# Filter spectra with half of the transforms, and the rest as sums and differences

## The reference

```python
z_pos, window = hyena_pos_features(L)
spec = hyena_filter_spectra(z_pos, window, hy_w1[i], hy_b1[i], hy_w2[i], hy_b2[i],
                            hy_w3[i], hy_b3[i], hy_freq[i])
y_b = hyena_mixer(hy, hy_conv[i], spec, hy_skip[i]) @ w_br_hyena[i]
```

## Time and profile before

| | |
|---|---|
| median of 3 runs | 2994.93 us (2990.47 to 2996.48) |
| profiled execution | 2988.92 us |
| its span | 2987.1 us |
| mean granted TensorE clock | 0.967 |
| TensorE, VectorE, ScalarE, GpSimd busy | 94%, 67%, 51%, 2% |
| stage `spectra` in the span | about 1634.8 to 1696.9 us |

### The profile page before, as it was taken

The page is one execution under the profiler, slowest core; times in us unless marked ns, Lnnn a source line. Parts: engine busy times, 40 slices in busy tenths (PEclk is TensorE's granted clock), DMA queues, the critical chain, the costliest instruction groups (busy, mean ns, idle before and its releaser), DMA issues. The chain is left out here.

```text
span 2987.1 us, 43738 instructions
## 1 busy us (share of the span) xinstructions
PE 2808.3 (94%) x17891; PEld 2482.1 (83%) x17891; DVE 2004.8 (67%) x2003; ACT 1514.4 (51%) x1456; POOL 68.8 (2%) x55
## 2 busy tenths in 40 slices
PE   5899998699999999999998989999899899989999
PEld 5799998588888888888886578999899788989898
DVE  6555565588888888888785466665555666666555
ACT  3444353466667676667663325444434326443442
POOL 1000000000000000000000210000000110000000
PEclk8899989699999999999999899999999999999999
DMA  6155540399999999999997234444355433444353
GB/s 188 61 180 192 177 155 16 121 365 331 368 329 349 347 334 364 328 366 334 340 356 233 94 97 127 142 155 142 113 178 190 147 111 102 150 147 141 127 186 110
DMA packets 365125, 619.40 MB, mean 207 GB/s; under 512 B 14664, under 2 KB 201127, under 8 KB 363701
## 3 DMA queue, kind: packets, MB, share of 16 engines
q1 hardware_dynamic: 363432, 611.77, 59.8%
q10 hardware_dynamic: 1550, 5.57, 0.5%
HBM read 611.93 MB, written 5.37 MB: 207 GB/s over the span
## 5 line engine op out<-in xcount | busy, mean ns | idle before, releaser
L366 DVE TENSOR_TENSOR slots_low<-slots,w_hi 128x2048 fp32r<-128x2048 f32 x240 | 549.5, 2293 | 379.4 <-ACT w_hi L355 379.2
L355 ACT ACTIVATE w_hi<-slots 128x2048 fp32r<-128x2048 f32 x240 | 452.8, 1891 | 335.9 <-PE ps L940 170.9
L1267 DVE TENSOR_TENSOR slots_low<-slots,w_hi 128x2048 fp32r<-128x2048 f32 x224 | 504.2, 2286 | 65.1 <-ACT w_hi L1218 65.1
L468 PE MATMUL ps<-x_hi,w_hi 128*128 128x256 f32 x1520 | 438.7, 289 | 51.5 <-DVE x_lo L548 26.7
L468 PE MATMUL ps<-x_lo,w_hi 128*128 128x256 f32 x1520 | 431.7, 284 | 0.0
L468 PE MATMUL ps<-x_hi,slots_low 128*128 128x256 f32 x1520 | 431.1, 284 | 0.0
L1218 ACT ACTIVATE w_hi<-slots 128x2048 fp32r<-128x2048 f32 x224 | 415.9, 1907 | 0.1
L1151 PE MATMUL ps<-slots_low,x_hi 128*128 128x512 f32 x896 | 352.1, 393 | 0.0
L468 PEld LDWEIGHTS ps<-x_hi,w_hi 128*128 128x128 f32 x1520 | 295.9, 195 | 59.4 <-issue 52.2
L468 PEld LDWEIGHTS ps<-x_lo,w_hi 128*128 128x128 f32 x1520 | 295.6, 194 | 0.3
L468 PEld LDWEIGHTS ps<-x_hi,slots_low 128*128 128x128 f32 x1520 | 295.3, 194 | 0.0
(11 more groups left out here) (536 smaller groups left out, 5374.0 us busy)
## 6 DMA issues: line engine op xcount, KB each, us to landing
slots<-in_moe_w_gate_dram SPq DMA_DIRECT2D x112, 1024.0 KB, 5.1
slots<-in_moe_w_up_dram SPq DMA_DIRECT2D x112, 1024.0 KB, 5.1
slots<-in_moe_w_down_dram SPq DMA_DIRECT2D x112, 1024.0 KB, 4.9
slots<-in_mlp_w_dram SPq DMA_DIRECT2D x64, 1024.0 KB, 5.2
slots<-in_w_in_dram SPq DMA_DIRECT2D x54, 1024.0 KB, 5.4
slots<-in_ffn_w_gate_dram SPq DMA_DIRECT2D x14, 1024.0 KB, 5.0
slots<-in_ffn_w_up_dram SPq DMA_DIRECT2D x14, 1024.0 KB, 5.0
slots<-in_ffn_w_down_dram SPq DMA_DIRECT2D x14, 1024.0 KB, 4.9
```

The costliest lines, as they stand in the source:

```text
L355: act.activation(w_hi[:, s.buffer, 0:s.kt * s.cols], slots[:, s.slot, 0:s.kt * s.cols], ACT.Copy).then_inc(w_hi_done, 1)
L366: dve.tensor_tensor(slots_low[:, s.slot, 0:n], slots[:, s.slot, 0:n], w_hi[:, s.buffer, 0:n].bitcast(F32), ALU.subtract).then_inc(w_lo_don ...
L468: mm = pe.matmul(b[:, t * T:(t + 1) * T], w, xx[:, k, :], **flags)
L1267: dve.tensor_tensor(low[i % NS], raw[i % NS], his[i % R].bitcast(F32), ALU.subtract).then_inc(lo_done, 1)
```

## The change

In a transform of the mirrored frequencies only the sign of the part over the odd (or even) tokens differs. The changed kernel no longer adds even and odd in a bank. `transform(i, s, t)` is one product for cosines or sines (s) over even or odd tokens (t), for the first 128 frequencies alone, into a bank of its own. ScalarE copies the even part of each into `evens`, which lies in the memory of `x_lo`, free in this stage. VectorE makes the sum and the difference of the odd part (in its bank) and the even part into `spectra` (`join`). `join(i, 0)` stands ahead of `mix(i + 1)` and of the size in VectorE's queue, `join(i, 1)` behind the size. The clearing of one row goes from VectorE to GpSimd, ahead of its addition.

```diff
-        xl = sb(ctx, "x_lo", [P, KD, T], F32R)
+        x_lo_plain, xl = pinned(ctx, "x_lo", [P, KD, T])
...
-                        def transform(i, n):
-                            s, k = n // 2, n % 2
+                        def transform(i, s, t):
                             pe.wait_ge(mixed, 2 * i + s + 1)
                             if i:
-                                pe.wait_ge(outed, 4 * (i - 1) + n + 1)
-                            for t in range(TT):
-                                mm = pe.matmul(bank(4 + n), dft[:, t, s, k * P:(k + 1) * P], pq[i % 2][:, s, t, :], start=(t == 0), stop=(t == TT - 1))
-                            mm.then_inc(transformed, 1)
+                                if t == 0:
+                                    pe.wait_ge(evens_out, 2 * (i - 1) + s + 1)
+                                else:
+                                    pe.wait_ge(joined, 4 * (i - 1) + 2 * s + 2)
+                            pe.matmul(bank(4 + 2 * s + t), dft[:, t, s, 0:P], pq[i % 2][:, s, t, :], start=True, stop=True).then_inc(transformed, 1)
...
                         def add_up(i):
                             pe.wait_ge(added, i + 1)
                             if i:
-                                pe.wait_ge(outed, 4 * i)
+                                pe.wait_ge(joined, 4 * i)
...
-                            transform(i, 0)
-                            transform(i, 1)
+                            transform(i, 0, 0)
+                            transform(i, 0, 1)
                             add_up(i)
-                            transform(i, 2)
+                            transform(i, 1, 0)
                             pe.wait_ge(sized, i + 1)
-                            transform(i, 3)
+                            transform(i, 1, 1)
...
-                            dve.wait_ge(windowed, 4 * i + 4)
-                            dve.memset(fb[0:1, 1, 0, :], 0.0).then_inc(lag0, 1)
...
+                        def join(i, s):
+                            if s == 0 and i:
+                                dve.wait_ge(spectra_out, 16 * i)
+                            dve.wait_ge(evens_out, 2 * i + s + 1)
+                            dve.wait_ge(transformed, 4 * i + 2 * s + 2)
+                            odd, even = bank(4 + 2 * s + 1), evens[:, s, :]
+                            dve.tensor_tensor(F[:, 2 * s, :], odd, even, ALU.add).then_inc(joined, 1)
+                            first, second = (even, odd) if s == 0 else (odd, even)
+                            dve.tensor_tensor(F[:, 2 * s + 1, :], first, second, ALU.subtract).then_inc(joined, 1)
...
                             if i + 1 < N:
                                 window(i + 1)
+                            join(i, 0)
+                            if i + 1 < N:
                                 mix(i + 1)
                             dve.wait_ge(summed, i + 1)
                             dve.tensor_scalar(filter_size[:, 1, 4 * i:4 * i + 4], bank(7)[:, 0:4], EPS, None, ALU.add).then_inc(sized, 1)
+                            join(i, 1)
...
                         for i in range(N):
+                            pool.wait_ge(windowed, 4 * i + 4)
+                            pool.memset(fb[0:1, 1, 0, :], 0.0).then_inc(lag0, 1)
                             pool.wait_ge(absd, 2 * i + 2)
...
                             if i + 1 < N:
                                 sizes(i + 1)
-                            if i:
-                                act.wait_ge(spectra_out, 16 * i)
-                            for n in range(4):
-                                act.wait_ge(transformed, 4 * i + n + 1)
-                                act.activation(F[:, n, :], bank(4 + n), ACT.Copy).then_inc(outed, 1)
-                            act.wait_ge(outed, 4 * i + 4)
+                            for s in range(2):
+                                act.wait_ge(transformed, 4 * i + 2 * s + 1)
+                                if i:
+                                    act.wait_ge(joined, 4 * (i - 1) + 2 * s + 2)
+                                act.activation(evens[:, s, :], bank(4 + 2 * s), ACT.Copy).then_inc(evens_out, 1)
+                            act.wait_ge(joined, 4 * i + 4)
                             act.dma_start(spectra_dram[l][o], flat(F[:, :, :])).then_inc(spectra_out, 16)
```

More of the change, by code:

```diff
@@ L1403, in spectra @@
                 F = sb(c, "spectra", [P, 4, 512])
+                evens = flat(x_lo_plain[:, 0:4, :]).rearrange("p (s n) -> p s n", s=2)
                 U = [(l, o) for l in range(2) for o in range(2)]
                 N = len(U)
-                with stage("made", "windowed", "lag0", "mixed", "absd", "added", "summed", "sized", "inverted", "transformed", "out") as \
-                        (block, made, windowed, lag0, mixed, absd, added, summed, sized, inverted, transformed, outed):
+                with stage("made", "windowed", "lag0", "mixed", "absd", "added", "summed", "sized", "inverted", "transformed", "evens_out", "joined") as \
+                        (block, made, windowed, lag0, mixed, absd, added, summed, sized, inverted, transformed, evens_out, joined):
                     @block.tensor
@@ L1458, in window, with mix @@
                                     dve.tensor_tensor(fb[:, d, t, :], bank(2 * d + t), win[:, t, :], ALU.mult).then_inc(windowed, 1)
-                            dve.wait_ge(windowed, 4 * i + 4)
-                            dve.memset(fb[0:1, 1, 0, :], 0.0).then_inc(lag0, 1)
+                        def mix(i):
                             dve.wait_ge(lag0, i + 1)
-                        def mix(i):
                             for n, op in enumerate((ALU.add, ALU.subtract)):
```

## The result

The changed kernel is slower: 3021.73 us (median of 6 runs, 3015.80 to 3025.76) against 2993.86 (6 runs), a ratio of 1.0097 with a 95% interval from 1.0084 to 1.0109. The forecast was 3017.4 with a range from 3004 to 3024. The profiled execution took 3015.80 us with a span of 3014.0, 26.9 more than before.

A forecast was written before the change was run, and what follows sets the result against it. TensorE was taken to set the stage's pace; the new queue order and low clock would move the stage's end from 1696.9 to 1719.4, +22.5 us on 2994.9, giving 3017.4 us, range 3004 to 3024.

The forecast's parts named there:

- The chain: After each unit's column sums: absolute values, even copy, first join, mix, size in series; TensorE idle 5 to 5.8 us.
- P+6.7: TensorE resumes 6.7 us after P, the moment it begins the product following a unit's column sums.
- The releaser: VectorE's size, named as what ends TensorE's idle wait at its fourth product of each unit.
- The clock: In middle units, low clock from the pause to the column sums: 12.0 us of TensorE work, period 21.3.
- the rival in which it comes back in them: Clock falls but returns during each unit's filters, 5.6 us after restart: +15 us, 3010; chance 12%.
- the one in which it never falls: Clock stays up because the idle stretch is split or bridged: period 14.4 us, +6.6, 3001.5; chance 8%.
- The rival in which TensorE stays the bound: Even copy reaches SBUF before the column sums end, so removed transforms pay: -13.7 us, 2981; chance 5%.
- First unit to P0: Filters as before, two products at the low clock, then sums of 1.7 to 3.4 us: P0 at 1654.0.
- Periods: Middle units: 6.7 us to resume, 12.0 at low clock, 2.6 of sums, 21.3 us each (bounds 20.4 and 22.1).
- Last period: From third to fourth unit's P, without further filters: 14.4 us, to P3 at 1711.0.
- End: After P3: last products, second join, then 4.3 us of store and barrier; 8.4 us in all, to 1719.4.
- The term that I set to nothing: VectorE's mix slowed beside GpSimd's sum: 0.1 us per unit on the overlap, taken as zero, 1.5 at the high end.

The follow-up runs named there:

- Two reorderings that break the chain at either end: Changed kernel with VectorE's size ahead of first join and mix: stage 61.57 us; or ScalarE's even copy ahead of the next absolute values: 58.75; changed kernel 85.24.
- the orders mended: Changed kernel with even copy ahead of absolute values and size between first join and mix: stage 57.49 us; with 90 empty products ahead, 48.53.
- the kernel with two buffers: Changed kernel with both queue reorderings, 90 empty products ahead in place of 50, and a second spectra buffer in x_hi: stage 43.14 us, ratio 0.9943.
- the row back: Changed kernel with the clearing of one row back on VectorE: stage 85.63 us, execution 27.3 us over the kernel before.
- pinned buffer: Kernel before with only the changed allocation of x_lo: stage 62.05 us, execution 4.7 us over the kernel before, ratio 1.0005.
- warm start: 90 empty products in place of 50 ahead of the stage: stage 53.56 us on the kernel before, 78.60 on the changed kernel.
- the pauses were filled: Changed kernel with 40 empty products in each of TensorE's three pauses: stage 71.97 us, execution 13.9 us over the kernel before.
- even copy first: Changed kernel with ScalarE's copy of the cosines' even part ahead of the next unit's absolute values: stage 58.75 us, 3.1 us below the kernel before.

## Why the prediction was right

**The chain.** P+6.7 was worked out for the end of the pause; measured is 7.03 in each of the three units (1655.86 to 1662.89, 1676.47 to 1683.50, 1697.01 to 1704.04). The 0.3 us more come from the mix, which took 0.5 longer beside GpSimd (below). The releaser is the one that was named. Two reorderings that break the chain at either end took 23.7 and 26.5 us off the stage.

**The clock.** It was 0.50 through the filters of units three and four, so the rival in which it comes back in them (12%) is out, and the one in which it never falls (8%) as well. The Trainium skill's rule on pauses between bursts ("TensorE: Matmul & The Clock Gate", section "HAM oscillation — how this bites in real kernels") agrees with this trace. The rule of the same page's section "Part 1: The HAM clock gate", that sustained matmul work gives the clock back, has to be read with care: 7.03 us of 65-row products after a pause did not, in the five profiles here that kept the pause empty, while the 128-row ones behind them did in the middle units. Nor did 13.8 us of 65-row products and 3.4 of 128-row ones in the first unit (0.50 up to 1655.86). Whether it is the rows was not tried by itself.

**The rival in which TensorE stays the bound** was excluded by the order of ScalarE's queue as written, not by any busy time. With the orders mended it is what happens in the middle units (a period of 8.66 us); its whole price of 13.7 us no run reached, the nearest is the 10.4 of the kernel with two buffers.

**The terms**, in the profiled execution, measured less forecast. First unit to P0: 20.47 after the first filter rather than 19.2 (+1.3: the sums took the whole 3.4 at the low clock, and the low clock took hold some 0.6 us earlier in the first filters). Periods 20.61 and 20.54 rather than 21.3 (-1.5 together: sums at 1.70, since the clock came back for them, against 0.5 more in the mix). Last period 13.69 rather than 14.4 (-0.7). End 9.93 rather than 8.4 (+1.5: the first join of the last unit waited for the store until 1711.42, and the last product ran at the low clock after 1.03 us of idle). Together +0.7: 23.2 in the stage where 22.5 was forecast. So the total is nearer than its parts: 2.8 us too little and 2.2 too much all but cancel, and that is luck. The term that I set to nothing and should not have is the mix beside GpSimd: 0.5 us per unit. I had taken the overlap of 0.5 us times the factor from the earlier trace rows; in the trace one mix instruction took up to 1.79 us rather than 1.22, as if it stood still while GpSimd worked. The Trainium skill says in "Advanced Engine Details and Errata", section "GPSIMD Details", that the two conflict where a VectorE instruction has two SBUF inputs; the trace agrees, and the joins, with one operand in PSUM, were not slowed (0.69 and 0.68 beside the addition, and the same without it at 1685.68).

**What stays open.** The change measured 27.9, 27.3 and 27.3 us (the changed kernel twice, and with the row back) where the stage explains 23.2 to 23.6. The forecast had no term for the rest; it fell inside the range, whose upper end is 2.3 us above the median. In the profiled executions the part behind the stage took 1290.2 us before, 1293.4 and 1300.9 in the two profiles of the changed kernel, and 1293.9 with the pinned buffer alone. Over the fourteen profiles it ran from 1290.2 to 1306.1 us, with 9200 matmul instructions in each, and TensorE's busy time in it from 1214.6 to 1233.6 while VectorE's stayed near 776: what varies is how long the matmuls take. The mean is 1297.6 in the eleven profiles with the change and 1293.2 in the three without it, which is about the amount that is missing. But the two kernels without the change that ran beside the one before (warm start, pinned buffer) also did 5.8 and 4.7 us worse in the execution than in the stage. Whether it is scatter or something systematic stays open.

## What to carry to other kernels

Count an engine's work to see whether a change can fit, but walk through every engine's queue in program order to see whether it does: here 3.4 us of TensorE work per unit were saved and a wait of 7 us was bought, because a 0.15 us result was queued behind a copy that stood behind another unit's work. A pause of TensorE has a second price, the slower products behind it, which was nearly as large as the pause itself (13.3 us of stage went when the pauses were filled, another 14.5 when they were gone). When a bound goes away, order the small results that others wait for first, and look next at single buffers whose store must land.

## What the runs showed of the hardware

Eight instructions of 65-row products right after an empty pause (7.03 us), and the 16 at the stage's start (13.8 us), did not bring the clock up, but 16 of them kept it up for 7.11 us where it was up before (warm start). 128-row products brought it up in the middle units of the changed kernel within the 3.2 us before the sums, and did not in the 3.4 us before the sums of the first unit. 40 small bf16 products of zeros (4.53 us) in a pause of 7 us were enough to keep it. Before the stage it was lost in, or just behind, 4.24 us without products; but the last product of the changed kernel was at 0.50 after only 1.03 us of idle (1.00 just before), while 1.17 and 1.20 us with the even copy first left it at 1.00. So the length of the pause alone does not tell.

VectorE's and GpSimd's two-input instructions on SBUF hold each other up, and the one that began first keeps its time: the mix of 128x1024 took up to 1.79 us rather than 1.22 behind an addition that had begun (2.35 us), and the addition took 2.93 rather than 2.35 us behind a mix that had begun.
